# A two-layer transformer kernel on one core: norm 1 of layer 1 and its Q, K, V products as one stage, a reordered tail of each layer, and value products on 64 output lanes in the attention

## The reference, cut to what matters

```python
for i in range(DEPTH):
    # six rows from silu(c) @ ada_w[i] + ada_b[i]: shift, scale, gate, twice
    n_lat = rms_norm(h_lat, norm1_g[i]) * (1 + sc1) + sh1      # and the same for the context
    if kind == 1:                                              # layer 1
        q, k, v = split(n @ w_qkv); q, k = rms_norm per head, rope on the latent ones
        s = q @ k.T * 64 ** -0.5                               # own block, two neighbours, context
        y = softmax([s, sink])[..., :-1] @ v @ w_o
    else:                                                      # layer 0
        y = fft2(n, axes=(token, feature in group)).real @ fnet_w + fnet_b
    h = h + g1 * y
    h = h + g2 * square(relu(modulate(rms_norm(h, norm2_g[i]), sh2, sc2) @ w1)) @ w2
```

## Time and profile before

| what | us |
| --- | --- |
| median of 3 runs (lowest, highest) | 2547.73 (2545.57, 2548.49) |
| the profiled execution | 2550.99 |
| its span | 2549.2 |
| TensorE busy | 2327.9 (91%) |
| VectorE busy | 1802.1 (71%) |
| ScalarE busy | 1137.3 (45%) |
| GpSimd busy | 955.8 (37%) |

### The profile page before, as it was taken

One profiled execution on the slowest core, in us unless ns is written; L12 is line 12 of the kernel. 1 busy time (PEld: TensorE's weight loads), 2 busy tenths in 40 slices (PEclk: granted clock), 3 DMA queues, 4 the chain that ended last, 5 costly groups with the idle time before them and its releaser, 6 DMA issues. The chain is left out here.

```text
span 2549.2 us, 37483 instructions
## 1 busy us (share of the span) xinstructions
PE 2327.9 (91%) x11646; PEld 1911.2 (75%) x11646; DVE 1802.1 (71%) x2955; ACT 1137.3 (45%) x2044; POOL 955.8 (37%) x698
## 2 busy tenths in 40 slices
PE   4988987999999999999679788885989999999998
PEld 2657776888888888888467566664868888888887
DVE  4552576777777777777777688884387778777776
ACT  4453542333333333333543488884343444434343
POOL 0003643334433344333400256553634445353544
PEclk9998988999999999999889899998999999999999
DMA  6434312222222122221121211103202111111102
GB/s 233 165 116 161 104 67 75 83 66 74 99 73 83 66 74 99 68 85 62 66 99 42 71 30 29 25 17 140 91 9 67 33 66 50 49 58 41 66 33 91
DMA packets 107590, 192.64 MB, mean 76 GB/s; under 512 B 40192, under 2 KB 50944, under 8 KB 104192
## 3 DMA queue, kind: packets, MB, share of 16 engines
q1 hardware_dynamic: 104304, 183.88, 21.7%
q10 hardware_dynamic: 3216, 7.86, 0.9%
HBM read 179.13 MB, written 12.58 MB: 75 GB/s over the span
## 5 line engine op out<-in xcount | busy, mean ns | idle before, releaser
L750 POOL TENSOR_TENSOR ht<-ht,l_side 128x512 f32<-128x512 f32 x224 | 301.1, 1344 | 940.9 <-ACT l_side L835 932.3
L1103 DVE SCALAR_TENSOR_TENSOR ht<-l_yy_ps,mod,ht 128x512 f32<-128x512 f32 x672 | 466.5, 743 | 29.2 <-PE l_yy_ps L1384 28.3
L51 PE MATMUL l_z_ps<-nh,l_w1h 128*128 128x512 f32 (+1 forms) x1280 | 474.2, 370 | 2.2 <-DVE nl L1044 2.2
L52 PE MATMUL l_z_ps<-nl,l_w1h 128*128 128x512 f32 (+1 forms) x1280 | 472.4, 369 | 0.0
L53 PE MATMUL l_z_ps<-nh,l_w1l 128*128 128x512 f32 (+1 forms) x1280 | 471.6, 368 | 0.0
L1382 PE MATMUL l_yy_ps<-l_ah,l_w2h 128*128 128x512 f32 x896 | 354.3, 395 | 2.7 <-DVE ht L1103 2.7
L1383 PE MATMUL l_yy_ps<-l_al,l_w2h 128*128 128x512 f32 x896 | 350.3, 391 | 0.0
L1384 PE MATMUL l_yy_ps<-l_ah,l_w2l 128*128 128x512 f32 x896 | 350.1, 391 | 0.0
L835 ACT ACTIVATE l_side<-l_yy_ps,mod 128x512 f32<-128x512 f32 x224 | 154.1, 688 | 343.8 <-PE l_yy_ps L1384 343.8
L51 PEld LDWEIGHTS l_z_ps<-nh,l_w1h 128*128 128x128 f32 x1280 | 242.2, 189 | 45.7 <-DVE nl L1044 4.7
L52 PEld LDWEIGHTS l_z_ps<-nl,l_w1h 128*128 128x128 f32 x1280 | 242.0, 189 | 40.5 <-issue 0.5
(11 more groups left out here) (213 smaller groups left out, 4550.1 us busy)
## 6 DMA issues: line engine op xcount, KB each, us to landing
l_w1f<-w SPq DMA_DIRECT2D x64, 512.0 KB, 3.4
l_w2f<-w SPq DMA_DIRECT2D x64, 512.0 KB, 4.8
l_aw<-ada SPq DMA_DIRECT2D x128, 256.0 KB, 2.9
maw<-ada SPq DMA_DIRECT2D x24, 1024.0 KB, 5.2
l_pf<-fnet_w SPq DMA_DIRECT2D x24, 512.0 KB, 3.5
qb<-queries SPq DMA_DIRECT2D x64, 128.0 KB, 2.7
l_pf<-wo SPq DMA_DIRECT2D x16, 512.0 KB, 3.5
l_x<-x SPq DMA_DIRECT2D x8, 512.0 KB, 5.8
```

The lines of the kernel that those rows point to most:

```text
L51: pe.matmul(out, lh, rh, start=first, stop=False)
L52: pe.matmul(out, lh, rl, start=False, stop=False)
L750: pool.tensor_tensor(h, h, side[(i - 1) % 2][:], ALU.add).then_inc(s_add, 1)
L1103: dve.scalar_tensor_tensor(out=h, in0=y_ps[m][:], scalar=mod[:, layer, G2, c, 0:1], in1=h, op0=ALU.mult, op1=ALU.add).then_inc(s_acc, 1)
```

## The change

It has four parts. In `layer_tail` of both layers the units follow a list `ORDER`. For layer 0 that is chunk m of blocks 0 and 2 in turn, both from one weight piece, then block 1: 16 pieces instead of 24. Piece 0 is the first load, the tiles of x are turned after the first units, the eight ada steps of the first pair run in every second of the first 16 units, blocks 0 and 2 get their means and norms during block 1's units, and the hidden tiles C0 and C1 come ahead of B12 and B22. For layer 1 the order of the units stays, and `mean(0)` comes one unit later.

```diff
+    ORDER = [(b, m) for m in range(KC) for b in ((0, 2) if C else (0,))] + [(1, m) for m in range(KC)]
+    WEIGHT = [m if b != 1 else KC + m for b, m in ORDER]
+    LATE = UNIT_AT[1, 0]
-    Z_FIRST = ["B11", "B21", "B12", "B22"] + (["C0", "C1"] if C else [])
+    Z_FIRST = ["B11", "B21"] + (["C0", "C1"] if C else []) + ["B12", "B22"]
-                if C:
-                    for t in range(4):
-                        tile(t)
                 for u in range(UNITS):
                     project(u)
-                    if u >= KC and u % KC == (0 if unit(u)[3] == 512 else 1):
-                        mean(u // KC - 1)
+                    for i in TILE_AT.get(u, []):
+                        tile(i)
+                    if u == LATE + (0 if C else 1):
+                        for b in MEANS[:-1]:
+                            mean(b)
...
+                    if C and u % 2 and u // 2 < STEPS:
+                        ada_step(0, slice(0, 1), u // 2)
```

```diff
+                def stats(b):
+                    for j in range(BLOCKS[b][1] // P):
+                        last = pe.matmul(COLS[b][:, j:j + 1], ssum[:, j * P:j * P + P], meanw[:, 0:1], start=True, stop=True)
+                def spread(b):
+                    for j in range(BLOCKS[b][1] // P):
+                        last = pe.matmul(rb_ps[b][:, j * P:j * P + P], meanw[:], dg[:, j], start=True, stop=True)
+                def norm(i):
+                    dve.scalar_tensor_tensor(out=tn[i % TN][:, 0:n], in0=ht[:, k, t0:t0 + n], scalar=mod[:, layer, SC1, k, version(b)],
+                                             in1=rb_ps[b][:, 0:n], op0=ALU.mult, op1=ALU.mult).then_inc(s_t, 1)
...
+                def post(u):   # GpSimd
+                    pool.tensor_tensor(y, y, m_[u % 2][:, 0:H * HD], ALU.add).then_inc(s_ym, 1)
...
+                        pool.tensor_tensor(y, y, r, ALU.mult).then_inc(s_fin, 1)
+                        pool.wait_ge(s_qh, u - KV + 1)
+                        pool.tensor_tensor(qhl[u % 2][:, :, 1, :], y, qhl[u % 2][:, :, 0, :], ALU.subtract).then_inc(s_ql, 1)
```

```diff
-                    pe.matmul(o[:], v, pth[slot][:], start=(kb == 0), stop=False)
-                    pe.matmul(o[:], v, ptl[slot][:], start=False, stop=(kb == KB - 1)).then_inc(s_o, 1)
+                    pe.matmul(o[0:HD, :], v[:, 0:HD], pth[slot][:], start=(kb == 0), stop=False)
+                    pe.matmul(o[0:HD, :], v[:, HD:2 * HD], pth[slot][:], start=False, stop=False)
+                    pe.matmul(o[0:HD, :], v[:, 0:HD], ptl[slot][:], start=False, stop=(kb == KB - 1)).then_inc(s_o, 1)
...
-                    for half in range(2):
-                        v = o_ps[n % 2][HD * half:HD * half + HD, :].rearrange("p (c s q) -> p c s q", c=2, s=2)
-                        for s in range(2):
-                            last = act.activation(ot[HD * s:HD * s + HD, half], v[:, :, s, :], ACT.Copy)
+                    for s in range(2):
+                        last = act.activation(nh[HD * s:HD * s + HD, c0:c0 + 2, cols], v[:, :, s, :], ACT.Copy)
...
-                    pool.tensor_tensor(of[:], ot[:, 0], ot[:, 1], ALU.add).then_inc(s_of, 1)
...
-                def part_q(jj, n):
-                    low = qs[n % 2][HD:P, :]
-                    dve.tensor_tensor(low, q_ps[HD:P, :], f32(low), ALU.subtract).then_inc(s_qs, 1)
```

More of the change, by code:

```diff
@@ new lines, in _ @@
+                for k in range(KC):
+                    square(k)
+                act.wait_ge(s_wkv, 16)
+                for k in range(KC):
+                    act.activation(weight(0, k)[0], wf_kv[:, k], ACT.Copy).then_inc(s_wkh, 1)
+                root(0)
+                for k in range(KC):
+                    normed(k)
+                    square(KC + k)
+                root(1)
+                for k in range(4):
+                    normed(KC + k)
+                    for j in (2 * k, 2 * k + 1):
+                        square(2 * KC + j)
@@ new lines, in _ @@
+                root(2)
+                post(0)
+                for k in range(4, KC):
+                    normed(KC + k)
+                post(1)
+                high(0)
+                for k in range(KC):
+                    normed(2 * KC + k)
+                    if k % 4 == 3:
+                        post(2 + k // 4)
+                for u in range(4, len(UNITS)):
+                    if u > KV:
+                        query(u - 1)
+                    post(u)
+                    if u in (6, 11, 16):
+                        high({6: 1, 11: 2, 16: 3}[u])
@@ new lines, in _ @@
+                for k in range(1, KC):
+                    add(k)
+                for k in range(KC):
+                    hi, lo = weight(0, k)
+                    dve.wait_ge(s_wkh, k + 1)
+                    lo_part(dve, lo, wf_kv[:, k], hi).then_inc(s_wkl, 1)
+                rstd(0)
+                for k in range(KC):
+                    norm(k)
+                    if k:
+                        low_n(k - 1)
+                    if k > 1:
+                        add(KC + k - 1)
+                low_n(KC - 1)
@@ new lines, in _ @@
+                add(2 * KC - 1)
+                rstd(1)
+                for k in range(4):
+                    norm(KC + k)
+                    for j in (2 * k - 2, 2 * k - 1):
+                        if j > 0:
+                            add(2 * KC + j)
+                for j in (KC - 2, KC - 1):
+                    add(2 * KC + j)
+                tables()
+                rstd(2)
+                post(0)
+                for k in range(4, KC):
+                    norm(KC + k)
+                post(1)
@@ L1705, in _ @@
                         pe.transpose(tr_ps[i % 2][:, 0:P], kr[:, kt, gg].rearrange("p a d -> p (a d)"), ident[:]).then_inc(s_tr, 1)
-def attention(nc, sem, sb, banks, masks, nsink, ident, qd, kh, kl, vs, nh, nl):
+                stats(0)
+                spread(0)
+                unit(0)
+                stats(1)
+                unit(1)
+                spread(1)
+                unit(2)
+                unit(3)
+                stats(2)
+                spread(2)
+                for u in range(4, len(UNITS)):
+                    unit(u)
@@ L1717, in attention @@
+def attention(nc, sem, sb, banks, masks, nsink, ident, qd, kh, kl, vs, nh, nl, mstore, qb, s_q, s_qb):
     PAIRS = QB // 2
@@ L1926, in whole_a @@
                         recip(jj, n)
[L1927 to L1929 removed]
+                schedule(dve, whole_a, lambda jj, n: None, step)
+                part_o(PAIRS - 1, NQ - 1)
             @block.tensor
```

932 lines of the change are left out of this document (513 added, 419 removed).

## The result

| what | before | after |
| --- | --- | --- |
| median, us (lowest, highest; runs) | 2546.88 (2545.57, 2548.49; 4) | 2525.01 (2523.15, 2528.41; 4) |
| ratio after / before (95% interval) | | 0.9913 (0.9897 to 0.9929) |
| profiled execution / its span | 2550.99 / 2549.2 | 2526.5 / 2524.6 |

The account below looks back on a forecast made before the run. TensorE, busy in 91% of the span, was taken as the bound, with waits in the attention. Gains of 25 + 15 + 11 - 5.4 = 45 us off the 2547.73 median gave 2503, range 2488 to 2518, outer range 2476 to 2536.

Parts of the forecast that it names:

- B: Norm, Q, K, V and handover: the attention's first transposes come at 1416 instead of 1430.78, gain 15 us.
- D: Layer 1's tail: the first mean, one unit later, delays the second mean and TensorE's hidden products, a loss of 5.4 us.
- C: Attention: steps fall from 9.62 to 9.3 us on average and the end shortens, gain 11 us.
- signs of being wrong: Attention steps above 9.6, a query pitch above 6.2, or a new wait on VectorE's norms at the projection's end.
- A: Layer 0's tail: earlier start, shorter projection and moved ada steps bring the first second-matrix product 25 us earlier.
- I leave that length as it is: Layer 0's tail: VectorE's chain of means, reciprocals, norms and splits still ends 41.0 us after the projection.
- rival 3: Layer 0's tail gains only 10, VectorE holding the projection back or the chain after it being longer: 2518; chance 0.15.
- The ring: Query units: each one's follow-up over ScalarE, VectorE and POOL (GpSimd) takes 5.75 us in all, five handovers included.
- rival 1: Query units: POOL's (GpSimd's) products hold VectorE's reduce, 14 us more, total 2517; chance 0.17.
- 1.0 more in every fourth: Attention: every fourth step, where mask and window's values change, takes 1.0 us more than the regular 9.07.
- rival 2: Attention: the waits close up and TensorE alone sets 8.7 us steps, gaining 28.5 instead of 10; total 2485; chance 0.12.
- Rival 4: Attention: the third value product stands wholly on the path, costing 62 us, total 2574, slower than before; chance 0.07.

Follow-up runs that it names:

- Experiment 8: Changed kernel with the context block's (block 2's) eight norms moved from layer 0's last two projection units to behind the last residual sum: 2521.25 us, ratio 0.9893.
- Experiment 7: Changed kernel with the first pair's eight ada steps and their loads back behind the hidden tiles: 2544.71 us, ratio 0.9986.
- Experiment 1: Changed kernel with the copies of the two masks and the window's values at the head of the step when the query block changes: 2499.26 us, ratio 0.9809.
- experiment 2: Changed kernel with 40 empty instructions on ScalarE ahead of the attention's loop: 2521.11 us, ratio 0.9892.
- experiment 3: Changed kernel with both the mask copies at the head of the step and the 40 empty ScalarE instructions: 2494.11 us, ratio 0.9788.
- experiment 6: Kernel before with only the attention's three value products on 64 lanes and direct way out, without GpSimd's sum: 2565.02 us, ratio 1.0068.
- experiment 9: Changed kernel with the first mean of layer 1 back behind project(8): 2521.84 us, ratio 0.9902.
- experiment 10: Changed kernel with ScalarE waiting for layer 1's first output weight piece before asking for the 4 MB parked stream: 2521.14 us, ratio 0.9898.

## Why the prediction was right and wrong

The 2525 lies within the outer range of 2476 to 2536, but outside the nearer one of 2488 to 2518, and no case that I had named came about as a whole. Of the four terms only B held, so that the total came out inside is owed to the width of the range; D's error also hid a third of C's. Two of the three signs of being wrong came: steps above 9.6, and a new wait at the end of the projection.

**A, 19.8 for 25.** The start and the end of the projection are within 1.1 and 0.1 us of the forecast, and the cover for the ada steps held. The 0.1 is partly luck: the terms that I listed (212.8, 110.2, ten tiles at 1.0, two means at 1.2, and 3) add up to 338.4 and not to 337.0. The step that failed is "I leave that length as it is": the 41.0 from the projection's end to the splits, forecast as 42.9 to the first second-matrix product, is 47.0. Experiment 8 puts 2.0 of these 4.1 on the norms of block 2, which fill VectorE in just the last units. Block 1 is now last, and its reciprocal of 512 columns takes 3.35 us where that of block 2 took 1.75; no run tests that order by itself. Another 1.3 us of the shortfall lie behind the first second-matrix product, and their cause stays open. This is rival 3's mechanism at a third of its price. I had named the wait as a sign (over 3 us before the modulation products) but not sized it. Experiment 7 shows the other term: the moved ada steps bring 19.7, where I had put 12.9 on them and 12.4 on the shorter projection. The two overlap, since without the move the modulation products come only 2.5 earlier, although the projection ends 12.6 earlier (336.74 for 349.35).

**B, 15.3 for 15.** Measured from the stage's start, the queries begin after 83.8 us (forecast 86.0) and end after 177.4 (176.5). The ring's 5.75 was met by 5.71, and rival 1 did not come: the reduce at 1384.14 takes 0.69 while GpSimd is at its product of 1383.70 (1.30 us, above), as long as without GpSimd (0.685), so it is not held. The Trainium skill's rule that the prediction weighed ("SBUF — State Buffer", section "Who interferes with whom", a reduce never contends on trn2) is borne out by that row.

**C, -12.8 for +11.** The regular step is 8.96 for 9.07, the third product's spacing 0.23 as taken, and no GpSimd sum or second pair of copies is in the way. The step that failed is "1.0 more in every fourth, where the mask and the window's values change": it is 3.2 to 4.5 more (12.2 to 13.4), 3.9 on average. I took two copies over as they were, at 0.22 each, though I had just taken away what kept GpSimd idle beside them, and though the Trainium skill's rule on the shared port stood in B's paragraph. Nor did I reckon with the clock that falls behind such a wait. Experiment 1 puts 29 us on both together. The second term, ScalarE's two gaps at each jump, was in neither sum nor rivals; the four steps at the jumps are 6.7 us longer than regular ones, and experiments 2 and 3 take 3 to 5 us off the attention. With both edits the attention gains 19.7, between my 11 and rival 2's 28.5: the 1.0 in every fourth step is not there either.

Rival 4 forecast a slower attention by another mechanism, the third product on the path; experiments 1 and 3 rule it out. But the slower outcome it warned of is what this part does on its own (experiment 6, 17 us slower).

**D, +2.3 for -5.4.** The mean's place costs 4.6 (experiment 9) for 5.4. What was missing is the start of layer 1's tail: the first product there comes 7.0 us sooner behind the issue of `wo` (9.6 for 16.6), in a kernel that asks for `wo` and the stream at nearly the same time. That this lead is the cause is argued from single traces (experiment 10) and not shown. I read the program there as unchanged, and so it is; what differs is by how much one queue is ahead of the other.

In sum the errors are -5 in A, -24 in C and +7.7 in D: 21.3 of the 22 between forecast and median.

## What to carry to other kernels

When an instruction is removed from an engine, ask what that engine does in its place, and what runs on the others at that moment: here a saved 0.74 us sum let four long GpSimd products start beside two 0.22 us copies, and that cost 3.2 to 4.5 us in each of seven places, TensorE's lost clock included. Put short copies that VectorE needs ahead of the instruction that releases GpSimd. Behind a loop's jump, compare the steps with the others; and let the small transfer that work waits for go out ahead of the large one.

## What the runs showed of the hardware that I had not expected

- A 128x128 VectorE copy of 0.22 us takes 1.28 beside GpSimd's 128x640 product, and two in a row 2.48.
- The same wait of 2.64 us on TensorE stands before a stretch at a granted clock of 0.87 on average in one step and of 1.00 in another; the first is 13.4 us long, the second 12.2.
- ScalarE gaps of 1.95 and 1.60 us behind a backward jump, with 29 instruction packets in the attention; 40 empty instructions ahead of the loop left 19 to 20 packets and about one gap of 1 us, and 120 brought one gap back, with 31 packets, and cost 4.5 us at the start. The rule behind it stays open.
- The same 512 KB piece was cast 13.1 us after its issue when 4 MB had been asked for 0.34 us earlier, 6.0 with 0.02 us between them, and landed in 3.8 alone. Experiment 6, with the lead of 0.34 us, had 13.3. That the lead alone makes the difference between 13 and 6 was not varied by itself.
